# A hybrid encoder layer on one core: eight plain tiles ahead of the Strassen pairs, T1 through DRAM, more casts on ScalarE

## What is computed

```python
h = x * (1 + sc2) + sh2
u = h @ w_up + b_up                                   # w_up: 1024 x 5632
uc = conv_b + sum(conv_w[j] * ctx[:, j:j + T] for j in range(3))   # ctx: two past rows, then u
a, g = split(uc, 2)
f = (a * gelu(g)) @ w_down                            # w_down: 2816 x 1024
x = layer_norm(ALPHA * x + g2 * f)
```

## Time and profile before

| what | value |
|---|---|
| median of three executions | 1892.29 us (1892.24 to 1895.44) |
| the profiled execution | 1895.71 us, its span 1893.9 us |
| TensorE | 1813.9 us busy, 96% of the span |
| VectorE, GpSimd, ScalarE | 60%, 46%, 32% |
| TensorE's mean granted clock | 0.981 of full speed |

### The profile page before, as it was taken

The page is one execution under the profiler, slowest core; times in us unless marked ns, Lnnn a source line. Parts: engine busy times, 40 slices in busy tenths (PEclk is TensorE's granted clock), DMA queues, the critical chain, the costliest instruction groups (busy, mean ns, idle before and its releaser), DMA issues.

```text
span 1893.9 us, 30909 instructions
## 1 busy us (share of the span) xinstructions
PE 1813.9 (96%) x12255; PEld 1737.0 (92%) x12255; DVE 1130.8 (60%) x2002; ACT 608.7 (32%) x1375; POOL 862.4 (46%) x605
## 2 busy tenths in 40 slices
PE   7999999999999999999999996889999999999984
PEld 6999888888999999899999996889999999999983
DVE  4837875773322324364345869675676668666687
ACT  3213444433222323342111685122222222322345
POOL 0332212212222222133336357297778778877851
PEclk9999999999999999999999998899999999999997
DMA  9443321114334334265333001011111111101112
GB/s 389 167 145 107 120 85 69 57 57 136 97 107 125 123 107 121 84 230 182 125 125 102 12 12 49 23 46 45 45 46 68 39 53 45 68 23 68 45 34 83
DMA packets 78903, 173.44 MB, mean 92 GB/s; under 512 B 9300, under 2 KB 42452, under 8 KB 78632
## 3 DMA queue, kind: packets, MB, share of 16 engines
q1 hardware_dynamic: 55112, 119.63, 18.8%
q10 hardware_dynamic: 23648, 51.84, 7.7%
HBM read 139.21 MB, written 32.24 MB: 91 GB/s over the span
## 4 chain that ended last, share of the span: by engine, by line
PE 84%; DVE 6%; POOL 2%; ACT 2%; DMA 2%; DVEq 2%; issue 2%; ACTq 0%; SPq 0%; POOLq 0%
PE acc L607 37%; PE px L889 12%; PE acc L889 7%; PE px L935 6%; PE acc L935 4%; PE px L854 2%; PE px L678 1%; PE acc L854 1%; PE px L878 1%; PE px L707 1%; PE px L690 1%; PE px L704 1%; PE px L780 1%; PE px L779 1%; PE px L778 1%
## 5 line engine op out<-in xcount | busy, mean ns | idle before, releaser
L607 PE MATMUL acc<-x_hilo_a,w_hilo 128*128 128x352 f32 x4032 | 664.3, 324 | 2.6 <-ACT x_c L1037 1.7
L607 PEld LDWEIGHTS acc<-x_hilo_a,w_hilo 128*128 128x128 f32 x4032 | 643.1, 188 | 10.8 <-issue 10.0
L485 POOL CAST w_hilo<-w_raw 128x1024 fp32r<-128x1024 f32 x73 | 84.8, 1162 | 732.7 <-PE acc L607 624.8
L510 POOL TENSOR_TENSOR w_unit<-w_raw,w_unit 128x512 fp32r<-128x512 f32 x116 | 171.5, 1478 | 70.6 <-ACT w_unit L1371 61.7
L487 POOL TENSOR_TENSOR w_hilo<-w_raw,w_hilo 128x1024 fp32r<-128x1024 f32 x73 | 189.0, 2589 | 5.8
L935 PE MATMUL px<-ffn_act,w_unit 128*128 128x352 f32 x900 | 152.0, 324 | 0.6 <-issue 0.5
L935 PEld LDWEIGHTS px<-ffn_act,w_unit 128*128 128x128 f32 x900 | 145.6, 189 | 1.6 <-issue 1.4
L889 PE MATMUL px<-x_hilo_a,w_unit 128*128 128x264 f32 x1128 | 145.2, 284 | 0.2 <-POOL w_unit L510 0.2
L1774 DVE SCALAR_TENSOR_TENSOR c_state<-c_state,stage,px 128x257 f32<-128x257 f32 x36 | 17.4, 482 | 206.9 <-PE px L780 206.9
L889 PEld LDWEIGHTS px<-x_hilo_a,w_unit 128*128 128x128 f32 x1128 | 140.5, 188 | 0.3 <-issue 0.3
L889 PE MATMUL px<-h_sums,w_unit 128*128 128x264 f32 x828 | 109.2, 287 | 3.5 <-POOL w_unit L510 3.5
...
## 6 DMA issues: line engine op xcount, KB each, us to landing
...
z_spill<-stage ACTq DMA_DIRECT2D x41, 528.0 KB, 2.7
...
stage<-z_spill ACTq DMA_DIRECT2D x20, 528.0 KB, 4.8
...
x_c<-in_x SPq DMA_DIRECT2D x8, 528.0 KB, 14.9
x_c<-in_x ACTq DMA_DIRECT2D x8, 528.0 KB, 4.0
```

Of the source, the lines that this page charges most:

```text
L485: nc.gpsimd.tensor_copy(to[:, 0, :], raw[:, s, :]).then_inc(w_hi, 1)
L510: nc.gpsimd.tensor_tensor(to[:, 1, :], src, to[:, 0, :].bitcast(F32), ALU.subtract).then_inc(w_ready, 1)
L607: last = mm(acc[:, n, 0:NW], whl[:, slot, wi, k * P:(k + 1) * P], rhs[:, xi, k, n * NW:(n + 1) * NW], start=(k == 0 and j == 0), stop=(k = ...
```

## The change

- Index 3 becomes two plain tiles (6 and 7), so that eight tiles precede d(0), and one pair follows it before d(1) instead of two. The pairs begin with 4.
- T1 is written to DRAM by a ScalarE-issued DMA when `sums_full` has it (four rows of 128x528), read back after the last plain tile over the dead columns of h, and split from there. `t1_full` is gone; `h2_full` of rows 2 and 3 waits for the first two stores.
- The residual is scaled by ScalarE (eight instructions of 128x1056) instead of VectorE.
- ScalarE also makes the high part of A11 in even pairs from 6 and in pair 21, right after `x_take` of the pair ahead. The odd pairs from 5 to 19, which follow a down, and pair 4 keep it on GpSimd.
- A new unit takes the slot of the unit that TensorE reads first, no longer that made five before.
- The order on ScalarE and VectorE around the plain tiles is rewritten.

```diff
@@ -67,16 +67,16 @@
 
-SINGLES = ((0, 0), (0, 1), (1, 0), (1, 1), (2, 0), (2, 1))
+SINGLES = tuple((pi, r) for pi in range(4) for r in range(2))
 NSING = len(SINGLES)
-PAIR0 = 3
+PAIR0 = 4
 
 
 def ffn_items():
 
     order = [("u", pi, r) for pi, r in SINGLES] + [("d", 0, 0), ("d", 0, 1)]
     for j in range(1, FF - 2):
-        order += [("p", j, 1), ("p", j + 1, 0), ("d", j, 0), ("d", j, 1)]
+        order += [("p", j, 1)] * (j > 1) + [("p", j + 1, 0), ("d", j, 0), ("d", j, 1)]
     order += [("p", FF - 2, 1), ("p", FF - 1, 0), ("p", FF - 1, 1)]
@@ -93,7 +93,29 @@
 UNIT_RING = [unit for unit in UNITS if unit[0][0] == "p" or unit[0][1] < FF - 1]
-UNIT_SLOT = {unit: r % NUNIT for r, unit in enumerate(UNIT_RING)}
+
+
+def terms(pi):
+
+    return "A11", "S2", "S1", "S3", "A12", "A22", "S4"
+
+
+def unit_places():
+
+    reads = [(item, part) for item in ITEMS[NSING:] for part in (terms(2 * item[1] + item[2]) if item[0] == "p" else (0, 1))]
+    slot, prev, held = {}, {}, {}
+    for r, unit in enumerate(UNIT_RING):
+        if r < NUNIT:
+            slot[unit], prev[unit] = r, None
+        else:
+            prev[unit] = min(held.values(), key=reads.index)
+            slot[unit] = slot[prev[unit]]
+        held[slot[unit]] = unit
+    return slot, prev
+
+
+UNIT_SLOT, UNIT_PREV = unit_places()
+LAST_SINGLE = {SLOT[P_FFN + i]: i for i in range(NSING)}
 
...
@@ -364,15 +383,23 @@
 
+        def after_down(pi):
+            return pi % 2 == 1 and PAIR0 < pi < 2 * FF - 2
+
+        def plain_parts(pi):
+            return ("A12", "A22") if pi == PAIR0 or after_down(pi) else ("A11", "A12", "A22")
+
+        def high_of(pi, part):
+            return sum(len(plain_parts(x)) for x in range(PAIR0, pi)) + plain_parts(pi).index(part) + 1
+
         def row_made(pi, r):
             return 2 * pi + 1 + (r if pi < PAIR0 else 1 - r)
 
         def unit_free(eng, unit):
-            r = UNIT_RING.index(unit)
-            if r < NUNIT:
-                eng.wait_ge(*ready(("u", *SINGLES[3 + r // 2], NT - 1)))
+            if UNIT_PREV[unit] is None:
+                eng.wait_ge(*ready(("u", *SINGLES[LAST_SINGLE[UNIT_SLOT[unit] // 2]], NT - 1)))
                 return
-            item, part = UNIT_RING[r - NUNIT]
+            item, part = UNIT_PREV[unit]
             if item[0] == "d":
...
@@ -501,8 +525,9 @@
                 count = UNIT_READY[unit]
-                if unit[1] in ("A12", "A22"):
-                    pool.wait_ge(a_hi, 2 * (2 * unit[0][1] + unit[0][2] - PAIR0) + (1 if unit[1] == "A12" else 2))
+                pi = 2 * unit[0][1] + unit[0][2]
+                if unit[1] in plain_parts(pi):
+                    pool.wait_ge(a_hi, high_of(pi, unit[1]))
                     pool.sem_inc(w_hi, 1)
...
@@ -576,6 +601,8 @@
                     split(P_FFN + 4 + kt // 2)
+            split(P_FFN + 6)
+            split(P_FFN + 7)
             for item in ITEMS[NSING:]:
...
@@ -1368,7 +1395,7 @@
                 unit_free(act, (item, part))
-                A(wu[:, UNIT_SLOT[item, part], 0, :], raw[:, p % 2, HALF:D], ACT.Copy).then_inc(a_hi, 1)
+                A(wu[:, UNIT_SLOT[item, part], 0, :], raw[:, p % 2, 0:HALF] if part == "A11" else raw[:, p % 2, HALF:D], ACT.Copy).then_inc(a_hi, 1)
 
@@ -1406,6 +1433,12 @@
 
+            def t1_store(kt):
+                act.dma_start(io["t1"][kt], hb[:, kt % 2, 0, 0:HN]).then_inc(ffn_dma, 16)
+
+            def t1_load(kt):
+                act.dma_start(XA[:, 1, kt, HN:T].bitcast(F32), io["t1"][kt]).then_inc(ffn_dma, 16)
+
             def full_rows(kt):
@@ -1413,6 +1446,7 @@
                     act.wait_ge(t34_lo, kt - 1)
+                    act.wait_ge(ffn_dma, 16 * 3)
                 for h in range(2):
@@ -1425,10 +1459,14 @@
                 A(tb[:, 2, 0, kt, :], h2[:, 0:HN], ACT.Copy).then_inc(ts_hi, 1)
+                t1_store(kt)
+
+            def residual_scale(k):
+                A(XC[:, k, :], XC[:, k, :], ACT.Identity, scale=der[:, 4, k:k + 1], bias=der[:, 5, k:k + 1]).then_inc(xc_rdy, 1)
 
             def t1_high(kt):
-                act.wait_ge(ts_rdy, KH + kt + 1)
-                A(XA[:, 0, kt, HN:T], t1_row(kt), ACT.Copy).then_inc(ts_hi, 1)
+                act.wait_ge(ffn_dma, 16 * (2 * KH + 2))
+                A(XA[:, 0, kt, HN:T], XA[:, 1, kt, HN:T].bitcast(F32), ACT.Copy).then_inc(ts_hi, 1)
 
...
@@ -1470,46 +1508,63 @@
             sums_high(1)
+            up_take(1, 2)
             h2_full(2)
-            up_take(1, 2)
-            h2_full(3)
             up_tap(0, 1)
-            sums_high(2)
-            sums_high(3)
             for n in range(NT):
                 up_take(2, n)
+            h2_full(3)
+            sums_high(2)
             up_tap(1, 0)
+            sums_high(3)
             ffn_gelu(0)
             for n in range(NT):
                 up_take(3, n)
             up_tap(1, 1)
+            for k in range(4):
+                residual_scale(k)
             act.wait_ge(t34_lo, KH)
             act.wait_ge(ts_lo, KH)
+            act.wait_ge(ffn_dma, 16 * (KH + 1))
             ffn_round(0)
             for n in range(NT):
                 up_take(4, n)
             ffn_gelu(1)
+            up_tap(2, 0)
             ffn_round(1)
-            up_tap(2, 0)
             for n in range(NT):
                 up_take(5, n)
             up_tap(2, 1)
-            act.dma_start(fcr[:, :, :, :], io["ffn_consts"]).then_inc(fc_in, 16)
+            act.dma_start(fcr[:, :, :, :], io["ffn_consts"]).then_inc(ffn_dma, 16)
+            for k in range(4, KT):
+                residual_scale(k)
+            for n in range(NT):
+                up_take(6, n)
+            ffn_gelu(2)
+            up_tap(3, 0)
+            for n in range(NT):
+                up_take(7, n)
+            for kt in range(KH):
+                t1_load(kt)
+            up_tap(3, 1)
             for kt in range(KH):
                 t1_high(kt)
-                if kt == 1:
-                    ffn_gelu(2)
-            act.wait_ge(fc_in, 32)
+            ffn_gelu(3)
+            plain_high(PAIR0, "A12")
             for pi in range(PAIR0, 2 * FF):
                 if pi > PAIR0:
+                    if not after_down(pi):
+                        plain_high(pi, "A11")
                     up_tap(pi - 1, 1)
                     up_tap(pi - 1, 0)
-                if pi % 2 and PAIR0 < pi < 2 * FF - 2:
-                    ffn_gelu(pi - 1)
-                plain_high(pi, "A12")
+                    if after_down(pi):
+                        ffn_gelu(pi - 1)
+                    plain_high(pi, "A12")
                 first_take(pi)
                 plain_high(pi, "A22")
-                if not (pi % 2 and pi < 2 * FF - 2):
+                if pi == PAIR0:
+                    ffn_round(2)
+                elif not after_down(pi):
                     ffn_gelu(pi - 1)
@@ -1917,27 +1972,14 @@
 
-            def residual_scale(kt):
-                for k in (kt, kt + KH):
-                    V.tensor_scalar(XC[:, k, :], XC[:, k, :], der[:, 4, k:k + 1], der[:, 5, k:k + 1], ALU.mult, ALU.add)
-
             def t2_low(kt):
                 dve.wait_ge(ts_hi, kt + 1)
                 V.tensor_tensor(tb[:, 0, 1, kt, :], hb[:, kt % 2, 1, HN:T], tb[:, 0, 0, kt, :].bitcast(F32), ALU.subtract).then_inc(ts_lo, 1)
 
-            def t1_full(kt):
-                if kt == 0:
-                    dve.wait_ge(*ready(("u", *SINGLES[NSING - 1], NT - 1)))
-                t1 = t1_row(kt)
-                V.tensor_tensor(t1, XA[:, 0, kt, HN:T].bitcast(F32), XA[:, 0, kt, 0:HN].bitcast(F32), ALU.subtract)
-                dve.drain()
-                V.tensor_tensor(t1, t1, XA[:, 1, kt, HN:T].bitcast(F32), ALU.add)
-                dve.drain()
-                V.tensor_tensor(t1, t1, XA[:, 1, kt, 0:HN].bitcast(F32), ALU.subtract).then_inc(ts_rdy, 1)
-
             def t1_low(kt):
                 dve.wait_ge(ts_hi, KH + kt + 1)
-                V.tensor_tensor(XA[:, 1, kt, HN:T], t1_row(kt), XA[:, 0, kt, HN:T].bitcast(F32), ALU.subtract).then_inc(ts_lo, 1)
+                V.tensor_tensor(XA[:, 1, kt, HN:T], XA[:, 1, kt, HN:T].bitcast(F32), XA[:, 0, kt, HN:T].bitcast(F32), ALU.subtract)\
+                 .then_inc(ts_lo, 1)
 
...
@@ -2045,50 +2089,46 @@
             sums_full(3)
+            ffn_conv(0, 1)
             t2_low(2)
-            ffn_conv(0, 1)
             t2_low(3)
-            residual_scale(0)
             ffn_conv(1, 0)
             ffn_prod(0)
-            residual_scale(1)
             ffn_conv(1, 1)
             ffn_low(0)
             ffn_prod(1)
-            residual_scale(2)
             ffn_conv(2, 0)
             ffn_low(1)
-            residual_scale(3)
+            ffn_conv(2, 1)
+            ffn_prod(2)
+            down_row(0, 0)
+            conv_first(3, 0)
+            down_row(0, 1)
+            t1_low(0)
+            t1_low(1)
             dve.drain()
-            conv_first(2, 1)
-            down_row(0, 0)
+            conv_second(3, 0)
+            down_row(0, 2)
```

(33 more changed lines are left out.)

15 lines of the change are left out of this document (8 added, 7 removed).

## The result

The changed kernel takes 1900.73 us (median of 6, 1900.02 to 1901.62), the kernel before 1893.34 us in the same comparison (median of 6, 1892.24 to 1895.44). The ratio is 1.0036, 95% interval [1.0024, 1.0048]: the change makes the kernel slower by 0.36%. (The ratios here are not the quotients of the medians; the two medians differ by 7.4 us.) The profiled execution took 1900.11 us, its span is 1898.3 us, 4.4 us more than that of before.

What follows compares the result with a forecast made beforehand. TensorE, busy 96% of the span, was taken to bound the kernel. The terms -25.8 + 22.3 + 8.0 + 0.4 = +4.9 us gave 1900.6 from the profiled 1895.7, 3.4 lower for the median: 1897 us, range 1874 to 1906.

Steps and rivals of the forecast that it cites:

- Part 1: Transition from tile 3's end to d(1): 99.3 us instead of 125.1, so 25.8 us less.
- tile 4: TensorE's stop ahead of plain tile 4: eviction moved earlier, weights end last, loss 1.8 us instead of 9.8.
- tile 5: Ahead of plain tile 5: TensorE waits 6.0 us for GpSimd's split, then a low-clock tail of 2.2 us.
- d(0), pair 4: First down and first pair: the stop ahead of d(0) and both GpSimd stops are gone.
- Part 2: A11 cast on ScalarE delays GpSimd's queue: new 2.8 us S2 stop in even pairs 6 to 20, 22.3 us in all.
- Part 3: Low clock behind the new S2 stops: five slow stretches of 1.6 us, 8.0 us; bounds 0 and 12.8.
- Part 4: The rest: pair 21's S2 stop 3.9 us instead of 3.5, +0.4; slot rule, residual scaling and tail nothing.
- the queue behind the late cast: GpSimd's in-order queue at S2; without meeting VectorE, a stop of 1.0 us, lower bound 8 us; as rival 1875 us, 12%.
- two meetings with VectorE: S2's last two GpSimd instructions run slow beside VectorE's tap, 1.52 and 2.19 us; without them 0.9 + 0.9 us less.
- The rival in which GpSimd slips behind VectorE: S2's sum starts behind the tap: three slow instructions, some 3.7 us a stop, all with tails; +17, 1909 us; 12%.
- The rival at full clock: The same 2.8 us stops in the alternation without low-clock tails: -3.1, 1889 us; 13%.

Runs made afterwards that it cites:

- The larger groups above: The kernel before, unchanged, run again on the chip of each group of follow-up runs: medians 1895.44, 1895.35 and 1895.42 us.
- The experiment with the evictions alone: Kernel before, six plain tiles kept, only ScalarE's evictions of tile 2 moved ahead of the last h row and the sums: 1894.77 us, ratio 0.9995.
- the short tap: Changed kernel with both instructions of VectorE's first tap in each even pair and pair 21 cut to 2 columns: 1876.46 us, ratio 0.9902.
- the half-tap run: Changed kernel with only the second instruction (L1991) of that VectorE tap cut to 2 columns, the first whole: 1886.23 us, ratio 0.9951.

## Why the prediction held

Forecast 1897 us, measured 1900.7; forecast +4.9 us in the profiled execution, measured +4.4. The 3.7 us between 1897 and 1900.7 are no part of the mechanism: 3.4 of them were taken off because the median of three executions of before lay that much below the profiled one. The larger groups above have their median at 1895.4, next to the profiled execution; without that step the forecast was 1900.6. Step by step:

| step | forecast us | measured us |
|---|---|---|
| Part 1, d(1) earlier | -25.8 | -28.25 |
| of it: tile 4 | 1.8 lost | 0.46 + 1.0 |
| of it: tile 5, stop and tail | 6.0 + 2.2 | 4.24 + 1.8 |
| of it: d(0), pair 4 | no stop | no stop |
| Part 2, eight S2 stops | 8 x 2.8 = 22.3 | 8 x 2.62 = 21.0 |
| Part 3, tails | 5 x 1.6 = 8.0 | 7 x 1.5 = 10.7 |
| Part 4, pair 21 | +0.4 | +1.4 |

That the sum came out within 0.5 us is in part luck: Part 1 gave 2.5 us more than forecast and the stops cost 1.3 less, while the tails cost 2.7 and pair 21 1.0 more.

**Part 1** was right in its mechanism and 2.5 us too careful. Tile 4 starts when its weights are there, 1140.8 as forecast (1141.0); the 1.0 in the table is tile 3's later end, behind a slower row after the LayerNorm (5.49 us at 1096.72, 4.25 before). The size that was off is tile 5: GpSimd finished its split at 1156.6 and not at 1158.6, because the last sum rows came earlier than I assumed. ScalarE's spill of T1 goes out as the row is there, beside the three casts of it and not behind them. ScalarE's timeline, with its DMA queue:

```profile
1129.93 0.65 ACT L1459 ACTIVATE h_sums<-h_full 128x528 fp32r<-128x528 f32 x1 [0.53 <-DVE h_full L1973]
1129.94 0.33 ACTq L1437 DMA_DIRECT2D t_spill<-h_full  x1
...
1133.44 2.98 ACT L1453 ACTIVATE h_full<-x_c,der 128x1024 f32<-128x1024 f32 x4 [1.21 <-DMA t_spill<-h_full]
```

Row 1's store lands 3.5 us after its issue (2.7 was allowed), but was issued 2 us earlier than I had it. Reading T1 back is hidden as forecast: issued at 1193.07, landed by 1198.3, and TensorE runs without a stop until 1236. The low activations of d(0) came at 1178.2 (forecast 1178). The experiment with the evictions alone shows that this order edit by itself gives nothing. That the time comes from the two plain tiles, which stand where TensorE had waited for VectorE's activations, while the order edits clear what would have stopped them, is read from the timelines; the tiles without the order edits, and the other order edits one by one, were not run.

**Part 2** held: the queue behind the late cast (0.83 us of the stop, shown by the short tap; its lower bound was put at 1.0) and two meetings with VectorE (0.9 each, shown one by one). That A11 is the cause is shown three ways: back on GpSimd, earlier on ScalarE, and alone in the kernel before. The rival in which GpSimd slips behind VectorE didn't happen: S2's sum started at 1619.66 and the tap at 1619.94, 0.28 us apart (0.27 in the working). The sum took its usual 1.29 us, and the tap 2.13; the cast that started while the tap ran took 1.52, of which 0.47 lie after the tap's end. The Trainium skill ("SBUF — State Buffer", "SBUF: two separate sides") calls the port pair an exclusive lock that whoever starts first holds for a whole instruction; these rows agree with it. But the prediction's reading that the same cast takes 0.6 or 1.5 us and never 1 doesn't hold for the whole trace: before, two casts took 0.81 and one 1.22, and the changed kernel has one of 0.97 (1207.28). By the rule a cast that comes late in the other instruction's time would wait only for the rest of it, so a value in between does not speak against it.

**Part 3** was sized too low: seven of eight, not five. Nothing in the working could tell five from seven; it was a count between none and eight by the nearest rows. From the start of the slow row to the next it is 4.52 us (1624.93 to 1629.45) where the half-tap run has 2.99: 1.53 us each. The rival at full clock (1889) is out.

**Part 4** had the right place and too small a size: +0.4 forecast, +1.4 measured. GpSimd's timeline at pair 21, the subtraction of A11 before and after the change:

```profile
1772.99 1.29 POOL L510 TENSOR_TENSOR w_unit<-w_raw,w_unit 128x512 fp32r<-128x512 f32 x1
```

```profile
1777.49 1.29 POOL L535 TENSOR_TENSOR w_unit<-w_raw,w_unit 128x512 fp32r<-128x512 f32 x1 [4.73 <-ACT w_unit L1398]
```

TensorE began the same row of 24 at 1771.53 before and at 1774.59 after, so the subtraction stands 1.46 us behind it and then 2.90: 1.44 later. From it to S2's end are 10.8 and 10.7 us. The whole of the 1.4 is thus the wait for ScalarE, which casts behind the rounding of the activation (it comes when VectorE has the product, after 12.33 us of idle time) and two evictions; I had taken GpSimd's wait for its panel to cover most of that.

The edits costed at nothing (slot rule, residual scaling) are nothing, each shown by a run, the slot rule with A11 on GpSimd. That T1 is kept rather than formed twice was not tried by itself; it is only read from the trace that its stores and loads end no stop of TensorE, and of ScalarE only the 1.21 us above and 1.74 us ahead of the high parts of T1 (1198.29).
